# A streaming hybrid trunk on one core: norms folded into their neighbour stages, keys, values and queries in one stage, and longer tile loads for the delta rule

## The chip, the cores and the metric

The kernel runs on one core of one Trainium2 chip. The metric is the device time of one execution in microseconds (us), the median of several runs. The profile is one execution of the same program.

## The reference

1024 prompt frames and 64 sample frames (1088 tokens, width 1024) go through two layers, in fp32. Cut to what matters here:

```python
def _rmsnorm(x, g):
    return x * rsqrt(mean(x * x) + EPS) * g

# layer 0: gated delta rule in chunks of 64 tokens, then a dense FFN
proj = _rmsnorm(x, norm_attn[0]) @ gdn_w_in          # conv, silu, l2norm give q, k, v; z, gates
sol = triangular_solve(a, rhs)                       # per chunk and head, 64 x 64
v_new = u - w @ S
o = (q * exp(g)) @ S + attn @ v_new
S = S * exp(g_last) + k.T @ v_new
x = x + (_rmsnorm(o, o_norm) * silu(z)) @ gdn_w_out
h = _rmsnorm(x, norm_ffn[0]);  x = x + (silu(h @ w1) * (h @ w3)) @ w2

# layer 1: sliding-window attention with one shared K/V, then a top-2-of-8 expert FFN
kv = _rmsnorm(x, kv_norm) @ w_kv                     # k is rotated
q = rope(_rmsnorm(x, norm_attn[1]) @ swa_w_q)
x = x + attend(q, k, v) @ swa_w_o
x = x + moe(_rmsnorm(x, norm_ffn[1]));  y = _rmsnorm(x, final_norm)
```

## The kernel before

The program is a row of stages; each allocates its own tiles and ends in a barrier of all engines. The activations stay in SBUF as `xT` (128 partitions, 8 tiles of 1088 tokens: feature by token). A product of a weight tile and the activations runs over three token blocks of 384, 384 and 320 columns into one PSUM bank each. Most products are `split_product` (line 178): weight and activations are each split in a rounded fp32r half and a remainder, and three fast passes are added (lines 182 to 184).

The stages in order: load, norm0, gates, projection, **delta**, mixout, tails, **norm1**, **ffnup**, ffndown, **norm2**, **kv heads**, values, **norm3**, **q heads**, attend, attout, norm4, routing, experts, final.

*Delta* (`delta_stage`) walks 17 chunks of 64 tokens in two chains of 4 head pairs. Every engine runs the same hand-written order of steps per chunk, `ORDER`, in which the steps x0, d0, x1, d1, vT and kT prepare the next chunk and R0 to R3 work on this one:

```python
ORDER = ("R0", "x0", "T", "d0", "R1", "x1", "R2", "d1", "R3", "vT", "N", "kT", "M")
```

x0 and x1 (PE line 1053) multiply the between-block scores `BT` with the solved triangular tile `TT`; d0 and d1 multiply the result with `TT` again (lines 1062 to 1064) and DVE subtracts it (line 1181). vT and kT turn v and k (lines 1072, 1079), R0 multiplies k and q with the state (line 1089), R1 to R3 make the new values, the new state and the output, and T gates the output of the chunk before. POOL scales the state (line 1030), copies gate columns (line 1022) and clears the next but one `TT` (line 1013). SP loads everything, in order: per tile of 128 tokens 16 DMAs for v, k (twice), q and z (`load_tile`, lines 933 to 937); per chunk 16 DMAs of 16x8x16 for the diagonal blocks of `TT` (line 962), one for `BT` (line 943) and one for the scores (line 949). `TT` and `BT` have two buffers each. Every second chunk the tile load stands ahead of the next solved tile:

```python
for c in range(NCHUNK):
    if c and c % 2 == 0:
        ...
        store_out(c // 2 - 1)
        if c // 2 + 1 < NT:
            load_tile(c // 2 + 1)
    if c + 2 < NCHUNK:
        load_solved(c + 2)
        load_between(c + 2)
        load_own(c + 2)
```

Before the first chunk DVE does the substitution of the last group of blocks (15 dependent pairs of small operations, lines 432 and 433); the result goes to DRAM and is loaded as the last chunk's `TT`.

*norm_stage* squares `xT` on ACT (line 272), adds pairs on DVE, sums over the partitions with a product by ones on PE (line 288), takes Ln and Exp on ACT, and DVE multiplies `xT` by gain and inverse norm (line 304). For ffnup it also splits the result in halves (lines 281 and 308); norm3 reuses norm2's inverse norm. *ffn_up_stage* loads two weight tiles per step (SP line 1289), POOL casts and splits them (lines 189, 191), PE does 44 products (two for each of 22 tiles), ACT takes Silu from PSUM (line 1320) and DVE multiplies it with the other product (line 1336). *add_product_stage* (mixout, ffndown, attout) splits its weights with ACT and POOL (lines 1411, 1388) and adds PSUM to `xT` on DVE (line 1439). *heads_stage* is called twice, 4 tiles for kv and 8 for q, with plain fp32 products (PE line 1501), whole weights loaded at its start (line 1481), ACT copying PSUM out (lines 1513, 1514), a product with a permutation for the rotation (line 1488), and DVE multiplying by cosine and sine (lines 1525 to 1530).

## Time and profile before

| what | us |
|---|---|
| runs (3) | 5010.85 to 5026.13, median 5025.32 |
| the profiled execution | 5010.89 |
| its span in the profile | 5009.2 |
| PE, DVE, ACT, POOL busy | 4260.1, 1897.7, 1629.8, 781.3 |
| delta stage, first load to last instruction | 829 to 1316 |
| norm1, from its first ACT instruction | 1563.0 |
| ffnup, first load to last product of DVE | 1604.7 to 2149 |
| norm2 to the start of attend | 2468.6 to 2767.9 |
| experts | some 3120 to 4960 |

An engine's busy time counts its instructions; waits, register work and DMA issue don't count. A timeline row has the start, the duration, the engine with its line and operation, the tiles, the count of merged instructions, and in brackets the idle time before it with what released it. SP's rows are the issue of DMAs on its queue, not their transfer. A row of busy time by stretch has the window, its length, the busy time of PE, PEld (weight loads), DVE, ACT and POOL with their instruction counts, then PEclk (TensorE's granted clock as a share of full speed), the busy share of the DMA engines and GB/s.

### The profile page before, as it was taken

The numbers are of one execution on the slowest core, as the hardware profiler recorded it, in microseconds if no ns is written. First come the engines' busy times: TensorE is split into PE (matmuls) and PEld (weight loads), VectorE is DVE, ScalarE is ACT, GpSimd is POOL, SyncE is SP. The second block draws the span as 40 slices with busy tenths as digits, with TensorE's granted clock in tenths as the row PEclk, the third lists the DMA queues.
The fourth block names the chain that finished last, engine by engine and source line by source line (L and its number), as shares of the span: only waits on it lengthen the run. The fifth ranks groups of instructions, "written<-read, shape, count | busy, mean of one in ns | idle before, by whom it ended". The sixth has DMA issues, their size and how long they took to land. (4 is left out here: it accounts for less than half of the span.)

```text
span 5009.2 us, 84182 instructions
## 1 busy us (share of the span) xinstructions
PE 4260.1 (85%) x33144; PEld 4016.5 (80%) x33144; DVE 1897.7 (38%) x2635; ACT 1629.8 (33%) x2867; POOL 781.3 (16%) x567
## 2 busy tenths in 40 slices
PE   3899995767695999979769677399999999999994
PEld 2889995756695999979736456399999999999993
DVE  3455664544312000011112542144545445455553
ACT  2573331433322000022200442153434344444441
POOL 0334310211132222223200112200000000000001
PEclk7999997988897999989879788599999999999996
DMA  1223587454432222134120012555656666666675
GB/s 51 65 69 96 140 221 174 119 119 114 126 115 58 66 64 64 52 117 124 55 59 6 0 30 74 156 154 157 171 168 171 173 179 175 184 186 182 177 209 178
DMA packets 1048767, 600.88 MB, mean 120 GB/s; under 512 B 184466, under 2 KB 1006195, under 8 KB 1048579
## 3 DMA queue, kind: packets, MB, share of 16 engines
q1 hardware_dynamic: 984114, 524.46, 37.9%
q10 hardware_dynamic: 55344, 46.60, 3.2%
q0 software_dynamic: 9120, 27.24, 1.7%
q8 instruction: 127, 2.08, 0.2%
q14 instruction: 62, 0.50, 0.0%
HBM read 498.56 MB, written 99.26 MB: 119 GB/s over the span
## 5 line engine op out<-in xcount | busy, mean ns | idle before, releaser
L2260 DVE TENSOR_TENSOR experts_w<-experts_raw,experts_w 128x1024 fp32r<-128x1024 f32 x352 | 415.2, 1220 | 152.7 <-ACT experts_w L2220 152.6
L182 PE MATMUL experts_pa<-experts_hx,experts_w 128*128 128x264 f32 (+6 forms) x1408 | 412.3, 293 | 9.5 <-DVE experts_w L2260 9.5
L183 PE MATMUL experts_pa<-experts_hx,experts_w 128*128 128x264 f32 (+6 forms) x1408 | 410.8, 292 | 0.0
L184 PE MATMUL experts_pa<-experts_hx,experts_w 128*128 128x264 f32 (+6 forms) x1408 | 409.8, 291 | 0.0
L182 PE MATMUL experts_pd<-experts_hid,experts_w 128*128 128x264 f32 (+6 forms) x1408 | 409.7, 291 | 0.0
L183 PE MATMUL experts_pb<-experts_hx,experts_w 128*128 128x264 f32 (+6 forms) x1408 | 409.3, 291 | 0.0
L182 PE MATMUL experts_pb<-experts_hx,experts_w 128*128 128x264 f32 (+6 forms) x1408 | 408.6, 290 | 0.0
L183 PE MATMUL experts_pd<-experts_hid,experts_w 128*128 128x264 f32 (+6 forms) x1408 | 408.4, 290 | 0.0
L184 PE MATMUL experts_pb<-experts_hx,experts_w 128*128 128x264 f32 (+6 forms) x1408 | 408.2, 290 | 0.0
L184 PE MATMUL experts_pd<-experts_hid,experts_w 128*128 128x264 f32 (+6 forms) x1408 | 408.1, 290 | 0.0
L182 PE MATMUL proj_pm<-hT,proj_w_hi 128*128 128x384 f32 (+1 forms) x1152 | 389.0, 338 | 19.7 <-POOL proj_w_lo L630 19.7
L184 PE MATMUL proj_pm<-hT,proj_w_lo 128*128 128x384 f32 (+1 forms) x1152 | 380.9, 331 | 0.0
L182 PE MATMUL ffnup_pm<-h_ffn,ffnup_w_hi 128*128 128x384 f32 (+1 forms) x1056 | 346.4, 328 | 39.7 <-POOL ffnup_w_lo L191 39.7
L183 PE MATMUL proj_pm<-hT,proj_w_hi 128*128 128x384 f32 (+1 forms) x1152 | 378.6, 329 | 0.0
L2220 ACT ACTIVATE experts_w<-experts_raw 128x1024 fp32r<-128x1024 f32 x352 | 351.9, 1047 | 16.2 <-DMA experts_raw<-in_moe_w 15.7
L184 PE MATMUL ffnup_pm<-h_ffn,ffnup_w_lo 128*128 128x384 f32 (+1 forms) x1056 | 348.6, 330 | 0.0
L183 PE MATMUL ffnup_pm<-h_ffn,ffnup_w_hi 128*128 128x384 f32 (+1 forms) x1056 | 346.9, 329 | 0.0
L2274 DVE TENSOR_TENSOR experts_w<-experts_raw,experts_w 128x1408 fp32r<-128x1408 f32 x128 | 202.3, 1622 | 199.3 <-ACT experts_w L2233 199.3
L182 PEld LDWEIGHTS experts_pa<-experts_hx,experts_w 128*128 128x128 f32 x1408 | 266.3, 189 | 10.0 <-DVE experts_w L2260 6.9
L183 PEld LDWEIGHTS experts_pa<-experts_hx,experts_w 128*128 128x128 f32 x1408 | 266.3, 189 | 0.0
L184 PEld LDWEIGHTS experts_pa<-experts_hx,experts_w 128*128 128x128 f32 x1408 | 266.2, 189 | 0.0
L184 PEld LDWEIGHTS experts_pb<-experts_hx,experts_w 128*128 128x128 f32 x1408 | 264.8, 188 | 0.0
(385 smaller groups left out, 10013.1 us busy)
## 6 DMA issues: line engine op xcount, KB each, us to landing
experts_raw<-in_moe_w SPq DMA_DIRECT2D x352, 512.0 KB, 4.7
experts_raw<-in_moe_w SPq DMA_DIRECT2D x128, 704.0 KB, 5.7
projected<-proj_out SPq DMA_DIRECT2D x48, 544.0 KB, 4.1
proj_w<-in_gdn_w_in ACTq DMA_DIRECT2D x48, 512.0 KB, 4.1
ffnup_w<-in_ffn_w SPq DMA_DIRECT2D x44, 512.0 KB, 5.0
ffndown_w<-in_ffn_w SPq DMA_DIRECT2D x32, 704.0 KB, 4.5
mixout_w<-in_gdn_w_out SPq DMA_DIRECT2D x32, 512.0 KB, 3.8
hidden<-ffnup_hid ACTq DMA_DIRECT2D x22, 544.0 KB, 2.7
```

The lines of the kernel that those rows point to most:

```text
L182: pe.matmul(out, as_r(w_hi), as_r(x_hi), start=first, stop=False)
L183: pe.matmul(out, as_r(w_hi), as_r(x_lo), start=False, stop=False)
L184: return pe.matmul(out, as_r(w_lo), as_r(x_hi), start=False, stop=last)
L2220: act.activation(as_r(w[:, u, 0, x, 0:KD, :]), raw[:, x, u, 0:KD, :], ACT.Copy).then_inc(rounded[x][u], 1)
L2260: dve.tensor_tensor(as_r(w[:, u, 1, x, 0:KD, :]), raw[:, x, u, 0:KD, :], w[:, u, 0, x, 0:KD, :], ALU.subtract).then_inc(split[x][u], 1)
L2274: dve.tensor_tensor(as_r(w[:, u, 1, x, :, :]), raw[:, x, u, :, :], w[:, u, 0, x, :, :], ALU.subtract).then_inc(split[x][u], 1)
```

## The change

1. **Delta.** v, q with k, and z of a tile become three DMAs of 1 MB; the first tile and the incoming states are issued from ACT's queue at the start of the stage. POOL copies v and k (k twice) per chain and chunk into the layouts that the transposes want. `TT` and `BT` get three buffers (`AHEAD`), and their loads are issued three chunks ahead. The substitution of the last group is spread, two steps per chunk over chunks 1 to 8, and its store moves to the pass of chunk 11 in SP's loop.
2. **Adding stages.** After each addition to `xT` DVE squares the sum and adds it to a tile `squares`.
3. **ffnup.** norm1 goes. `inverse_norms` sums `squares` over the partitions on PE, ACT takes the root, DVE the reciprocal. ACT rounds `xT` times gain and DVE makes the remainder; the inverse norm is multiplied in when DVE takes the products out of PSUM. The first step of PE's loop is written out with waits for each split tile.
4. **Heads.** norm2 and norm3 go. kv and q are one stage of 12 tiles with `split_product`; POOL multiplies the weights by the gain, ACT rounds them, POOL makes the remainder; DVE multiplies by the inverse norm on the way out of PSUM. Weights come tile by tile, in two buffers.

The diff, cut to its core:

```diff
 # delta_stage
-        BT = st.sb("BT", [P, 2, L, HK, CHUNK])
-        TT = st.sb("TT", [P, 2, 2, HK, CHUNK])
+        BT = st.sb("BT", [P, AHEAD, L, HK, CHUNK])
+        TT = st.sb("TT", [P, AHEAD, 2, HK, CHUNK])
...
+            def load_tile(eng, t):
+                par, n = t % 2, TILES[t][1]
+                for to, first, loaded in ((v, 2 * HK, v_loaded), (qk, 0, qk_loaded), (z, 2 * HK + HV, z_loaded)):
+                    eng.dma_start(to[:, par, :, 0:n], proj[first:first + HV, :, t * P:t * P + n].rearrange("h p t -> p h t")).then_inc(loaded[par], 16)
...
+                load_between(0)
                 load_solved(0)
...
+                load_between(2)
+                load_solved(2)
+                load_tile(sp, 1)
                 for c in range(NCHUNK):
...
                         if c // 2 + 1 < NT:
-                            load_tile(c // 2 + 1)
+                            load_tile(sp, c // 2 + 1)
...
+                    if c + AHEAD < NCHUNK:
+                        load_between(c + AHEAD)
+                        load_solved(c + AHEAD)
                     if c + 2 < NCHUNK:
-                        load_solved(c + 2)
-                        load_between(c + 2)
                         load_own(c + 2)
...
+                    t = tile(c)
+                    pool.wait_ge(v_loaded[t], landed(c))
...
+                    pool.tensor_copy(vst[ch][:, c % 2, :, :], v[:, t, HC * ch:HC * ch + HC, cols(c)]).then_inc(e["v_staged"], 1)
+                    pool.wait_ge(qk_loaded[t], landed(c))
+                    pool.tensor_copy(kst[ch][:, c % 2, :, :, :], qk[:, t, HK + PAIRS * ch:HK + PAIRS * ch + PAIRS, cols(c)].unsqueeze(2).broadcast_to([P, PAIRS, 2, CHUNK])).then_inc(e["k_staged"], 1)
...
+                load_tile(act, 0)
+                for ch in C:
+                    act.dma_start(S[ch][:, 1, :, :], io["state_delta"][0, 0, HC * ch:HC * ch + HC].rearrange("h k v -> k h v")).then_inc(sems[ch]["state_loaded"], 16)
...
-                substitute(dve, step, blocks, solved, terms, 1)
...
+                    substitute(dve, step, blocks, solved, terms, 1, 2 * c - 1, min(2 * c + 1, SUB))
 # inverse_norms (new)
+        for b, (c, n) in enumerate(BLK):
+            last = pe.matmul(bank[:, b, 0:n], m["const"][:, C_ONES * P:(C_ONES + 1) * P], m["squares"][:, c:c + n], start=True, stop=True)
...
+            last = act.activation(root[:, c:c + n], bank[:, b, 0:n], ACT.Sqrt, bias=m["eps"][:, :], scale=1.0 / D)
...
+        dve.reciprocal(rinv[:, :], root[:, :]).then_inc(inverted, 1)
 # ffn_up_stage, ACT and DVE
+                for k in range(KD):
+                    act.activation(as_r(hT[:, 0, k, :]), m["xT"][:, k, :], ACT.Copy, scale=by_gain(k)).then_inc(x_rounded, 1)
+                    if k == 1:
+                        roots(act)
...
+                    dve.scalar_tensor_tensor(out=as_r(hT[:, 1, k, :]), in0=m["xT"][:, k, :], scalar=by_gain(k), in1=hT[:, 0, k, :],
+                                             op0=ALU.mult, op1=ALU.subtract).then_inc(x_split, 1)
+                    if k == 3:
+                        invert(dve)
...
+                    dve.tensor_tensor(two, rtwo, pm[:, x, 0:2, 0:384], ALU.mult)
+                    dve.tensor_tensor(rest, rrest, pm[:, x, 2, 0:320], ALU.mult).then_inc(scaled_now, 1)
 # add_product_stage, DVE
+                    dve.tensor_tensor(sq[:, :].rearrange("p (b t) -> p b t", b=2), to, to, ALU.mult).then_inc(squared, 1)
...
+                    dve.tensor_tensor(own, own, sq[:, :], ALU.add).then_inc(gathered, 1)
 # heads_stage, POOL, PE and ACT
+                    pool.tensor_tensor(w[:, u, :, :], w[:, u, :, :], m["gains"][:, gain:gain + KD].unsqueeze(2).broadcast_to([P, KD, P]), ALU.mult).then_inc(w_gained[u], 1)
+                    pool.wait_ge(w_rounded[u], PRE + t // 2 + 1)
+                    pool.tensor_tensor(as_r(w_lo[:, u, :, :]), w[:, u, :, :], w_hi[:, u, :, :], ALU.subtract).then_inc(w_split[u], 1)
...
+                            last = split_product(pe, pm[:, u, b, 0:n], w_hi[:, u, k, :], w_lo[:, u, k, :], xs[:, 0, k, c:c + n], xs[:, 1, k, c:c + n], k == 0, k == KD - 1)
...
+                    act.activation(as_r(xs[:, 0, k, :]), m["xT"][:, k, :], ACT.Copy).then_inc(x_rounded, 1)
+                    if k == 0:
+                        weights(0)
+                    if k == 1:
+                        roots(act)
```

Three places in the order of the instructions. On SP, in the loop over the chunks of the delta stage, the end of one tile load and what follows it, before:

```order
L933 DMA delta_vst<-projected 128x8x64
L935 DMA delta_kst<-projected 128x4x64 x2
L933 DMA delta_vst<-projected 128x8x64
L935 DMA delta_kst<-projected 128x4x64 x2
L936 DMA delta_qst<-projected 128x4x128
L937 DMA delta_zst<-projected 128x8x128
L962 DMA delta_TT<-solved_blocks 16x8x16 x16
L943 DMA delta_BT<-between_blocks 128x1024
L949 DMA delta_attn<-own_scores 128x512
L962 DMA delta_TT<-solved_blocks 16x8x16 x16
L943 DMA delta_BT<-between_blocks 128x1024
L949 DMA delta_attn<-own_scores 128x512
```

Here the block pieces of the next tile stand behind the whole tile load. The same place in the change, one pass of two chunks:

```order
L968 DMA gated_outputs<-delta_out 128x8x128 x2
L935 DMA delta_v<-projected 128x16x128
L935 DMA delta_qk<-projected 128x16x128
L935 DMA delta_z<-projected 128x16x128
L944 DMA delta_BT<-between_blocks 128x1024
L963 DMA delta_TT<-solved_blocks 16x8x16 x16
L950 DMA delta_attn<-own_scores 128x512
L944 DMA delta_BT<-between_blocks 128x1024
L963 DMA delta_TT<-solved_blocks 16x8x16 x16
L950 DMA delta_attn<-own_scores 128x512
```

Eight of the sixteen tile DMAs show in the first piece; the three in the second are a whole tile, and `BT` now stands ahead of the sixteen pieces, which belong to a chunk further on.

On POOL, two chunks of the delta stage before (`delta_S` is the state, `delta_cst` the gate columns):

```order
L1030 TENSOR_TENSOR delta_S<-delta_S,glast 128x1024 x2
L1022 COPY delta_cst<-cols 128x20 x2
L1013 MEMSET delta_TT 128x1024
L1030 TENSOR_TENSOR delta_S<-delta_S,glast 128x1024 x2
L1022 COPY delta_cst<-cols 128x20 x2
L1013 MEMSET delta_TT 128x1024
```

That is three kinds of work per chunk. One chunk of the same loop in the change:

```order
L1041 TENSOR_TENSOR delta_S<-delta_S,glast 128x1024 x2
L1025 COPY delta_cst<-cols 128x20
L1031 COPY delta_vst<-delta_v 128x512
L1033 COPY delta_kst<-delta_qk 128x512
L1025 COPY delta_cst<-cols 128x20
L1031 COPY delta_vst<-delta_v 128x512
L1033 COPY delta_kst<-delta_qk 128x512
L1016 MEMSET delta_TT 128x1024
```

Four copies per chunk stand between the state's scaling and the clearing of a `TT`.

On DVE, the end of norm1 and the head of ffnup's loop before:

```order
L304 SCALAR_TENSOR_TENSOR norm_h<-xT,gains,norm_rinv 128x1088
L308 TENSOR_TENSOR h_ffn<-norm_h,h_ffn 128x1088
L304 SCALAR_TENSOR_TENSOR norm_h<-xT,gains,norm_rinv 128x1088
L308 TENSOR_TENSOR h_ffn<-norm_h,h_ffn 128x1088 x2
L265 UNCONDITIONAL_BRANCH
L1327 UNCONDITIONAL_BRANCH
L1329 UNCONDITIONAL_BRANCH
L1329 ISA
L1332 ISA
L1333 ISA
L1336 TENSOR_TENSOR ffnup_hid<-ffnup_silu,ffnup_pm 128x768
L1337 TENSOR_TENSOR ffnup_hid<-ffnup_silu,ffnup_pm 128x320
```

The loop has one step, two instructions, per tile. The same place in the change:

```order
L1404 SCALAR_TENSOR_TENSOR h_ffn<-xT,gains,h_ffn 128x1088 x4
L1316 RECIPROCAL ffnup_rinv<-ffnup_root 128x1088
L1404 SCALAR_TENSOR_TENSOR h_ffn<-xT,gains,h_ffn 128x1088 x4
L1409 UNCONDITIONAL_BRANCH
L1409 ISA
L1412 REGISTER_ALU
L1399 TENSOR_TENSOR ffnup_scaled<-ffnup_rinv,ffnup_pm 128x768
L1400 TENSOR_TENSOR ffnup_scaled<-ffnup_rinv,ffnup_pm 128x320
L1414 REGISTER_ALU
L1399 TENSOR_TENSOR ffnup_scaled<-ffnup_rinv,ffnup_pm 128x768
L1400 TENSOR_TENSOR ffnup_scaled<-ffnup_rinv,ffnup_pm 128x320
L1419 ISA
```

The multiplications by the inverse norm have moved behind the products, and a reciprocal of 128x1088 stands in the middle of the splits.

## Rows read from the trace of the kernel before

**Rows 1.** Busy time by stretch: delta's start, delta, ffnup.
```profile
829.00:882.00 53.00, 11.52 (x176) 10.83 (x176) 12.05 (x38) 1.54 (x4) 2.99 (x6) 0.55 0.90 191
882.00:1316.00 434.00, 313.47 (x5675) 283.13 (x5673) 203.78 (x402) 171.70 (x677) 82.47 (x81) 0.88 0.48 114
1618.00:2152.00 534.00, 529.20 (x3168) 528.94 (x3166) 29.72 (x44) 39.20 (x55) 135.91 (x42) 1.00 0.20 62
```

**Rows 2.** PE's waits by line, delta stage: us in total, times, longest.
```profile
PE delta_bank_x L1053 <- issue: 104.8, 15, 14.7
```

**Rows 3.** Timeline of PE, delta stage: start, us, instruction, [idle before <-releaser].
```profile
840.30 1.97 PE L1053 MATMUL delta_bank_x<-delta_TT,delta_BT 64*64 64x64 f32 x32 [27.68 <-DMA delta_BT<-between_blocks]
...
845.02 0.45 PE L1062 MATMUL delta_bank_x<-delta_X,delta_TT 64*64 64x64 f32 x4
...
875.52 1.98 PE L1053 MATMUL delta_bank_x<-delta_TT,delta_BT 64*64 64x64 f32 x32 [29.83 <-DVE delta_TT L1181]
...
882.55 1.09 PE L1089 MATMUL delta_bank_w<-delta_S,delta_kst 128*64 128x128 f32 x16 [0.28 <-DVE delta_kd L1194]
...
900.44 1.09 PE L1089 MATMUL delta_bank_w<-delta_S,delta_kst 128*64 128x128 f32 x16
...
919.91 1.09 PE L1089 MATMUL delta_bank_w<-delta_S,delta_kst 128*64 128x128 f32 x16
...
957.61 1.97 PE L1053 MATMUL delta_bank_x<-delta_TT,delta_BT 64*64 64x64 f32 x32 [14.63 <-issue]
...
1297.86 1.09 PE L1089 MATMUL delta_bank_w<-delta_S,delta_kst 128*64 128x128 f32 x16
```

**Rows 4.** Timeline of SP's queue, delta stage.
```profile
928.69 1.36 SPq L933 DMA_DIRECT2D delta_vst<-projected  x1
...
945.79 8.05 SPq L962 DMA_DIRECT2D delta_TT<-solved_blocks  x16
```

**Rows 5.** Timelines of ACT, SP, POOL and PE around norm1 and ffnup.
```profile
1563.00 4.11 ACT L272 ACTIVATE norm_sq<-xT 128x1088 f32<-128x1088 f32 x4 [18.36 <-PEq L144]
...
1604.70 20.32 SPq L1289 DMA_DIRECT2D ffnup_w<-in_ffn_w  x8
...
1610.87 1.89 POOL L189 CAST ffnup_w_hi<-ffnup_w 128x2048 fp32r<-128x2048 f32 x1 [63.76 <-DMA ffnup_w<-in_ffn_w]
...
1617.46 0.68 PE L182 MATMUL ffnup_pm<-h_ffn,ffnup_w_hi 128*128 128x384 f32 x1 [39.74 <-POOL ffnup_w_lo L191]
```

**Rows 6.** Timelines of ACT, PE and DVE, norm2 to attend.
```profile
2468.55 4.11 ACT L272 ACTIVATE norm_sq<-xT 128x1088 f32<-128x1088 f32 x4 [18.59 <-PEq L144]
...
2511.90 20.11 PE L1501 MATMUL kv_pm<-h_att,kv_w 128*128 128x384 f32 x60 [27.61 <-DMA kv_w<-in_w_kv]
...
2577.10 0.73 DVE L1537 COPY vTt<-kv_raw 128x1088 f32<-128x1088 f32 x1 [13.83 <-ACT kv_raw L1514]
...
2597.56 10.19 DVE L304 SCALAR_TENSOR_TENSOR h_att<-xT,gains,rinv_att 128x1088 f32<-128x1088 f32 x8 [5.34 <-PEq L144]
...
2646.39 1.99 PE L1488 MATMUL q_pm<-q_raw,const 128*128 128x384 f32 x6
...
2767.87 0.63 ACT L1733 ACTIVATE attend_qs<-qT 128x512 f32<-128x512 f32 x1 [8.62 <-PEq L144]
```

**Rows 7.** Timeline of DVE, start of the delta stage.
```profile
865.40 0.16 DVE L432 TENSOR_TENSOR delta_terms<-delta_solved,delta_blocks 128x1 f32<-128x1 f32 x1 [36.76 <-DMA delta_blocks<-score_blocks]
```

**Rows 8.** Groups by line and shape, whole span: busy us, mean ns | idle.
```profile
L630 POOL TENSOR_TENSOR proj_w_lo<-proj_w,proj_w_hi 128x1024 fp32r<-128x1024 f32 x48 | 148.6, 3096 | 184.2 <-ACT proj_w_hi L656 183.0
...
L1388 POOL TENSOR_TENSOR mixout_w_lo<-mixout_w,mixout_w_hi 128x1024 fp32r<-128x1024 f32 x32 | 76.2, 2385 | 167.1 <-ACT mixout_w_hi L1411 167.1
...
L1705 POOL COPY attend_ks<-kT 128x384 f32 x12 | 7.7, 640 | 112.0 <-PE attend_scores L1653 112.0
...
L405 DVE RECIPROCAL gates_beta<-gates_beta 128x144 f32<-128x144 f32 x1 | 1.1, 1054 | 0.0
...
L1336 DVE TENSOR_TENSOR ffnup_hid<-ffnup_silu,ffnup_pm 128x768 f32<-128x768 f32 x22 | 21.0, 954 | 516.7 <-PE ffnup_pm L184 516.7
```

More of the change, by code:

```diff
@@ L423, in _, with substitute @@
                         dve.tensor_copy(rows[:, a, s:s + n], pchan[0:HV, b, 0:n]).then_inc(emptied, 1)
-def substitute(dve, step, blocks, solved, terms, groups):
-    for i in range(1, SUB):
+def substitute(dve, step, blocks, solved, terms, groups, first=1, end=SUB):
+    for i in range(first, end):
         t = terms[:, 0:groups * i * i].rearrange("p (g c j) -> p g c j", c=i, j=i)
@@ L1099, in v_new @@
                     for i, hp in both:
-                        last = pe.matmul(b_w[ch][rows(hp), i, :], TT[rows(hp), par, 1, PAIRS * ch + i, :], vb[ch][rows(hp), i, :], start=True, stop=True)
+                        last = pe.matmul(b_w[ch][rows(hp), i, :], TT[rows(hp), slot, 1, PAIRS * ch + i, :], vb[ch][rows(hp), i, :], start=True, stop=True)
                     last.then_inc(e["vn_summed"], 1)
@@ L1301, in _, with product @@
             def _(pe):
-                with pe.Fori(0, KF // 2) as i:
+                def product(i, u, x, freed, done, first=False):
+                    pe.wait_ge(freed, PRE + 2 * i + u)
+                    for k in range(KD):
+                        if first:
+                            pe.wait_ge(x_split, PRE + k + 1)
+                        for b, (c, n) in enumerate(BLK):
+                            last = split_product(pe, pm[:, x, b, 0:n], w_hi[:, u, x, k, :], w_lo[:, u, x, k, :], hT[:, 0, k, c:c + n], hT[:, 1, k, c:c + n],
+                                                 k == 0, k == KD - 1)
+                    last.then_inc(done, 1)
@@ new lines, in _ @@
+                dve.wait_ge(inverted, PRE + 1)
+                dve.wait_ge(rope_l, PRE + 16)
+                for t in range(HEAD_TILES):
+                    dve.wait_ge(done, PRE + t + 1)
+                    if not rotated(t):
+                        dve.sem_inc(copied, 1)
+                        scale(vT[:, t - KV_T, :], t).then_inc(ready, 1)
+                        continue
+                    if t >= 2:
+                        dve.wait_ge(ready, PRE + t - 1)
+                    scale(raw(t), t).then_inc(copied, 1)
+                    dve.wait_ge(copied, PRE + t + 1)
+                    dve.wait_ge(turned, PRE + rotations(t) + 1)
+                    two, rest = blocks3(sn)
+                    stwo, srest = blocks3(rope[:, 1, :])
+                    dve.wait_ge(ready, PRE + t)
+                    dve.tensor_tensor(two, stwo, pm[:, t % 2, 0:2, 0:384], ALU.mult)
+                    dve.tensor_tensor(rest, srest, pm[:, t % 2, 2, 0:320], ALU.mult)
+                    step(dve.tensor_tensor(raw(t), raw(t), rope[:, 0, :], ALU.mult))
+                    for to, c in dests(t):
+                        n = to.shape[-1]
+                        last = dve.tensor_tensor(to, raw(t)[:, c:c + n], sn[:, c:c + n], ALU.add)
+                    last.then_inc(ready, 1)
```

378 lines of the change are left out of this document (214 added, 164 removed).

## Prediction

> **What bounds the kernel now.** I read four views in this order: busy time by stretch, the PE waits by line in the delta stage, and then the timelines of the engines where one stage hands over to the next.
>
> By stretch [rows 1] the stages differ. In the up projection PE is busy 529 of 534 us at a granted clock of 1.00, so that stage can only lose its start or its end: 529.20 us over 3168 matmuls is 0.167 us each, and the 72 of one product take **12.03 us**. In the delta stage PE is busy 313 of 434 us, DVE 204, POOL 82, and the DMA engines 0.48 of the time: nothing there is full, so something waits in line. Of the waits of that stage [rows 2] one dominates: 104.8 us, in 15 pieces of up to 14.7 us, in front of the first between-block product (L1053), with no releaser that the profile names.
>
> The PE timeline [rows 3] shows where. R0 of successive chunks (L1089, the mark I count periods with) starts at 882.55, 900.44, 919.91; then the L1053 product at 957.61 has waited 14.63. From the first R0 to the last at 1297.86 there are 16 periods in 415.31 us, 25.96 each, while the undisturbed one from 900.44 to 919.91 takes 19.47. SP [rows 4] explains it: at 928.69 it starts the small loads of the next tile (16 DMAs) and only at 945.79 the 16 block pieces of the solved tile, 8.05 us of issue, without which L1053 can't start. 945.79 + 8.05 is 953.84, and a few us of landing later PE goes on, at 957.61. SP's issue, 17.1 us for one tile, is the wait.
>
> The norms are serial [rows 5, 6]. Norm1 starts at 1563.00, the first weight DMA of the up stage goes out at 1604.70 and PE's first product at 1617.46, so 54.5 us pass without a product. From norm2 at 2468.55 to attend at 2767.87 there are 299.3 us: two norms, loads of weights that nothing covers (PE waits 27.61 before its first product there, at 2511.90), and 12 tiles at fp32.
>
> **The change part by part.**
>
> *Delta, the start.* x0 runs at 840.30 now; it waits for the same transfers afterwards. Its update ends at 845.47 (the last d0 group starts at 845.02), and DVE's subtraction follows in some 0.7 us. Today x1 waits till 875.52, 29.83 us on DVE [rows 3], because DVE first has the substitution of the last group, which itself waits 36.76 us for its blocks [rows 7] and runs from 865.40 to about 874.5. Without it x1 could run at 846.7 and R0 7.03 us later, at 853.7 (from 875.52 to 882.55). What is late next is the tile: v and qk, 2 MB, come from ACT's queue beside SP's loads. At the 191 GB/s of this stretch [rows 1], half of it for ACT, 2 MB land some 22 us after 829, at 851, and the copies, the transposes and the scaling of k come behind. I take R0 at 856, with bounds 853.7 and 865: **−26.5** (−28.9 to −17.6).
>
> The rule that would speak against moving these loads is in the Trainium skill, Trainium Kernel Development and Optimization, Key Constraints: DMAs of all issuing queues share the same 16 engines, and another queue saves issue time only. The DMA share of 0.90 in this stretch [rows 1] agrees. By that rule alone the start keeps its bytes, only their order helps, and the gain would be the lower end, −17.6, in place of −26.5.
>
> *Delta, the periods.* SP's queue for a pair of chunks now holds 2 stores, 3 loads, and twice BT, 16 pieces and attn, and the pieces are those of three chunks ahead. Issue of the pieces is 2 × 8.05; with some 5 us for the rest that is 21 of two periods' 38.9 us, so SP is no limit, and one chunk more of lead covers the landing. I take 19.47 for each of 16 periods, 311.5: **−103.8**. Ends: the first period, 17.89 (882.55 to 900.44; it lacks the gate of an earlier chunk, so I don't take it), −129; and 20.5, one more us of staging in every period, −87.
>
> *What is added there.* POOL copies v and k for both chains, 4 of 128x512 per chunk. The nearest row is a copy of 128x384 at 640 ns [rows 8], so 0.85 each, 3.4 per chunk, at most 6 if the broadcast of k is dear. POOL is busy 82 of 434 us, 4.9 per chunk; 8.3 of 19.5 is covered. The copies stand behind the two state scalings in POOL's order, and a late tile would hold the scalings and the clearing of the next chunk; PE needs v only in the last third of a chunk. The substitution becomes at most 1.8 us per chunk in 8 chunks of DVE, which is busy 204 of 434: **0**. Without that cover it costs its 9.1 us.
>
> *The up projection's start.* Its weight load moves from 1604.70 to norm1's place, 1563.00: **−41.7** [rows 5]. From load to first product stay 12.8 us. In that time ACT rounds 8 tiles (norm1's four took 4.11 us), PE sums the squares and DVE splits 8 (1.35 each, 954 × 1088/768 [rows 8]) with the reciprocal of 128x1088 after four. That one has a row only as 128x144 at 1054 ns [rows 8]: × 1088/144 is **8.0 us**. The last split comes about 1583; PE, from 1575.7 at 1.5 us per k and slower at first, would want it at about 1586. So the first product should hardly stall; I take 2, with ends 0 and 12 (the reciprocal in full and half as much again). The squares add 1.5 behind the last addition (two 128x544 operations at 954 × 544/768 = 0.68, and a hand-over), and the extra eviction step 1.4 behind the last product. Inside the loop the evictions run beside the other bank's product, some 4.1 of every 24 us of DVE, free. Sum: −41.7 + 2 + 1.5 + 1.4 = **−36.8** (−39 to −27).
>
> *Keys, values and queries.* From the old 2468.55: 1.5 for the squares; first weights 0.5 MB, about 4.8 us (two such take 6.17 in the up stage, 1604.70 to 1610.87), then POOL's gain 2.39, ACT's rounding of some 1.1 and POOL's difference 2.39 [rows 8], 11 in all; the first tile 20, since ACT's rounding of the weights stands in front of its later x tiles and the reciprocal falls into it; 11 more tiles × 12.03 = 132.3, three fast passes in place of fp32; 9 swaps of 2.0 [rows 6] = 18; behind the last product scaling, swap and rotation 7.5; and the values stage with its barriers as now, 2577.83 to 2597.56 [rows 6], 19.7. Sum 210.0 against 299.3: **−89.3** (−99 to −72). Each tile's weights take about 11 us to prepare, beside the 14 us of the tile ahead.
>
> *The attention output* also gathers squares, which nobody reads: **+1.5**.
>
> Sum: −26.5 − 103.8 − 36.8 − 89.3 + 1.5 = **−254.9**. On the profiled execution, 5010.9 us: 4756. The median of the three runs lies 14.4 above that, the lowest run at it; I put the forecast about midway, **4762 us**.
>
> **The rivals.**
>
> *The long waits stay.* No row names the releaser of the 104.8 us; that it is SP's issue is my reading of two timelines. Were it the landing of the transfers, or did the 3 MB now ahead of the pieces in the queue hold them, −103.8 would go: 4866. Against it: a DMA share of 0.48, and the sum 953.84 plus landing. 8 in 100.
>
> *POOL and DVE take turns at the stage starts.* The same subtraction of 128x1024 takes POOL 3096 ns in the projection, where DVE is busy, and 2385 in the mix output [rows 8]: so a cost of 0.7 each is seen. If at both starts POOL (6.6 in the up stage, 1610.87 to 1617.46 [rows 5], 4.8 in the heads) and DVE (eight splits of 1.35 each) ran one after the other, and the reciprocal came on top, up to 11 us each time and 6 for a clock that falls meanwhile: +28, 4790. 9 in 100. The Trainium skill, SBUF — State Buffer, Who interferes with whom, states such a rule: a VectorE operation with two SBUF inputs and a GpSimd operation that reads SBUF hold a shared port for the whole instruction. The 0.7 us of those rows agrees in sign and shows no full turn.
>
> *TensorE falls to 1.2 GHz.* Now the evictions of the up stage go through one more engine step. If PE waited for each, its granted clock could stay at the lower of its two levels and a product take up to twice as long: 44 × 12.03 = +529, 5291. It decides the sign from 21 slow products on (255/12). Against it: two PSUM banks, 4.1 of 24 us, and a clock of 1.00 now. 2 in 100; this is the case on the slow side.
>
> **How the numbers follow.** My forecast has 81 in 100, the three rivals 8, 9 and 2. The forecast's own ends, all costs at their better or worse bounds, are some −45 and +50, and not all at once: 4762 − 44 to 4762 + 58, **4718 to 4820**, takes in the second rival and leaves out the first and third, and perhaps one tenth more for several terms off together. Faster by over 0.3% (15 us, about what a measurement tells from no change): 0.97; within it 0.01; slower 0.02.
>
> **What would show it.** Right: R0 every 19.5 us, no wait of over 2 us before the first between-block product, R0 first near 856; the up stage's first weight DMA at the end of the tails stage and the first product 13 us later; heads at 14 us per rotated tile. Wrong: a pair of a long and a short period; PE waiting for POOL's copies or for DVE's reciprocal for more than a few us; a granted clock under 0.9 in the up stage.

## The result and the profile after

| | before | changed |
|---|---|---|
| median of 4 runs (us) | 5024.62 | 4770.62 |
| lowest and highest | 5010.85, 5026.13 | 4744.34, 4783.22 |
| profiled execution | 5010.89 | 4772.82 |

The ratio is 0.9497, with a 95% interval of 0.9473 to 0.9521: 5% faster. One execution of those reported below (the kernel before with attend filled, 6091.88 us at a mean granted clock of 0.676) was in a slow state and counts in no ratio. The forecast was 4762 in 4718 to 4820. Six marks in the two profiled executions show where the 238.0 us of their spans come from (starts in us; the first two columns are rows, the others differences):

| mark | before | changed | earlier by | gained since the mark above | forecast |
|---|---|---|---|---|---|
| first R0 of delta | 882.55 | 857.06 | 25.5 | 25.5 | 26.5 |
| last R0 | 1297.86 | 1154.78 | 143.1 | 117.6 | 103.8 |
| last addition of ffndown | 2465.30 | 2287.83 | 177.5 | 34.4 | 36.8 |
| attend's first ACT instruction | 2767.87 | 2501.95 | 265.9 | 88.4 | 89.3 |
| attout's first weight DMA | 2955.48 | 2714.24 | 241.2 | **−24.7** | 0 |
| end of the span | 5009.2 | 4771.2 | 238.0 | −3.2 | −1.5 |

Everything up to attend gained 9.5 us more than forecast; attend, which the change doesn't touch, gave back 24.7.

Busy time by stretch of the changed kernel (delta's start, delta, ffnup; columns as in [rows 1]):

```profile
831.00:857.00 26.00, 8.95 (x176) 7.92 (x176) 4.58 (x10) 1.53 (x4) 7.14 (x11) 0.64 1.11 258
857.00:1174.00 317.00, 297.78 (x5672) 269.54 (x5672) 221.24 (x432) 168.89 (x677) 119.22 (x144) 0.99 0.61 153
1436.00:1969.00 533.00, 530.29 (x3168) 529.77 (x3167) 107.08 (x116) 38.62 (x33) 155.82 (x42) 1.00 0.20 61
```

The delta stage takes 317 us in place of 434, and PE is busy 298 of them at a clock of 0.99, not 0.88. Its work is the same, so of the 117 us some 16 are PE's own time at the higher clock (313.5 us before, 297.8 now), which came with the end of the long waits; the rest was waiting. ffnup is as full as before: 530 of 533 us. PE's two largest waits in delta, which answer [rows 2]:

```profile
PE delta_bank_x L1064 <- DMA delta_TT<-solved_blocks: 31.1, 1, 31.1
PE delta_bank_w L1083 <- DVE delta_o L1233: 5.6, 32, 0.2
```

The 104.8 us ahead of the first between-block product are gone; what is left is the wait for the first pieces at the start. PE's timeline in delta, against [rows 3]:

```profile
847.21 1.98 PE L1064 MATMUL delta_bank_x<-delta_TT,delta_BT 64*64 64x64 f32 x32 [31.14 <-DMA delta_TT<-solved_blocks]
...
857.06 1.09 PE L1102 MATMUL delta_bank_w<-delta_S,delta_qk 128*64 128x128 f32 x16 [0.23 <-issue]
...
874.97 1.09 PE L1102 MATMUL delta_bank_w<-delta_S,delta_qk 128*64 128x128 f32 x16
...
893.67 1.09 PE L1102 MATMUL delta_bank_w<-delta_S,delta_qk 128*64 128x128 f32 x16
...
1154.78 1.09 PE L1102 MATMUL delta_bank_w<-delta_S,delta_qk 128*64 128x128 f32 x16 [0.16 <-issue]
```

R0 now comes every 18.6 us (297.72 over 16), mostly every 18.43. SP's queue: the first load of the tile ahead of it, then one whole tile load, against [rows 4]:

```profile
861.25 0.44 SPq L935 DMA_DIRECT2D delta_v<-projected  x1
...
902.50 1.36 SPq L935 DMA_DIRECT2D delta_v<-projected  x1
903.90 4.07 SPq L935 DMA_DIRECT2D delta_qk<-projected  x1
908.01 3.47 SPq L935 DMA_DIRECT2D delta_z<-projected  x1
911.58 3.49 SPq L944 DMA_DIRECT2D delta_BT<-between_blocks  x1
915.11 9.73 SPq L963 DMA_DIRECT2D delta_TT<-solved_blocks  x16
```

Here is the first thing that the prediction had wrong: three DMAs and `BT` keep SP from 902.50 to 915.07, 12.6 us, not some 5. The issue of a megabyte with only small pieces just ahead of it took 0.44 us (861.25); the second and third megabyte of a tile took 1.8 to 5.0 us each in this stage. Still nobody waits, because the pieces belong to a chunk three further on.

The start of ffnup, on ACT, SP, POOL, DVE and PE, against [rows 5]:

```profile
1421.56 2.29 ACT L1381 ACTIVATE h_ffn<-xT,gains 128x1088 fp32r<-128x1088 f32 x2 [21.31 <-PEq L144]
...
1422.19 73.70 SPq L1341 DMA_DIRECT2D ffnup_w<-in_ffn_w  x12
...
1428.16 1.89 POOL L189 CAST ffnup_w_hi<-ffnup_w 128x2048 fp32r<-128x2048 f32 x1 [25.09 <-DMA ffnup_w<-in_ffn_w]
1430.13 5.43 POOL L191 TENSOR_TENSOR ffnup_w_lo<-ffnup_w,ffnup_w_hi 128x2048 fp32r<-128x2048 f32 x1
...
1422.79 2.62 DVE L1404 SCALAR_TENSOR_TENSOR h_ffn<-xT,gains,h_ffn 128x1088 fp32r<-128x1088 f32 x2 [5.74 <-ACT h_ffn L1381]
1428.17 8.54 DVE L1404 SCALAR_TENSOR_TENSOR h_ffn<-xT,gains,h_ffn 128x1088 fp32r<-128x1088 f32 x2 [2.77 <-ACT h_ffn L1381]
1436.63 6.94 DVE L1316 RECIPROCAL ffnup_rinv<-ffnup_root 128x1088 f32<-128x1088 f32 x1
...
1435.62 0.69 PE L182 MATMUL ffnup_pm<-h_ffn,ffnup_w_hi 128*128 128x384 f32 x1 [10.07 <-POOL ffnup_w_lo L191]
...
1444.80 0.45 PE L182 MATMUL ffnup_pm<-h_ffn,ffnup_w_hi 128*128 128x384 f32 x1 [0.76 <-DVE h_ffn L1404]
```

From the load to PE's first product are 13.4 us (forecast 12.8). Two splits take 2.62 us at 1422.79 and 8.54 at 1428.17, and these end at 1436.71, one split's time behind the end of POOL's subtraction at 1435.56: the rows fit engines that took full turns. The reciprocal takes 6.94 us (estimated at 8.0). PE waits just 0.76 for a split, since it has four to work on meanwhile. But its first product starts when POOL's subtraction ends, and that took 5.43 us where the kernel before has

```profile
1612.84 4.49 POOL L191 TENSOR_TENSOR ffnup_w_lo<-ffnup_w,ffnup_w_hi 128x2048 fp32r<-128x2048 f32 x1
```

The heads stage, from its start to attend, against [rows 6]:

```profile
2293.66 1.11 ACT L1651 ACTIVATE x_halves<-xT 128x1088 fp32r<-128x1088 f32 x1 [21.18 <-PEq L144]
...
2302.86 0.69 PE L182 MATMUL heads_pm<-x_halves,heads_w_hi 128*128 128x384 f32 x1 [5.38 <-POOL heads_w_lo L1613]
...
2316.58 0.69 PE L182 MATMUL heads_pm<-x_halves,heads_w_hi 128*128 128x384 f32 x1 [5.43 <-DVE x_halves L1671]
...
2324.99 0.95 DVE L1666 TENSOR_TENSOR qT<-heads_rinv,heads_pm 128x768 f32<-128x768 f32 x1 [4.87 <-PE heads_pm L184]
...
2501.95 0.63 ACT L1891 ACTIVATE attend_qs<-qT 128x512 f32<-128x512 f32 x1 [8.78 <-PEq L144]
```

The first product starts 9.2 us into the stage (forecast 11) and the first tile takes 22.1 (forecast 20), with a wait of 5.43 for a split behind the reciprocal. By mark, 88.4 of the forecast 89.3.

Attend, before and changed, in the same columns as [rows 1]:

```profile
2767.87:2955.48 187.61, 131.59 (x1312) 85.49 (x1312) 106.75 (x272) 96.38 (x372) 21.65 (x49) 0.81 0.00 0
```

```profile
2502.00:2714.24 212.24, 163.22 (x1312) 105.48 (x1312) 109.82 (x273) 96.64 (x373) 20.20 (x49) 0.63 0.00 0
```

The same 1312 matmul records take 131.6 us of PE in one and 163.2 in the other; the granted clock is 0.81 and 0.63, and the stage 187.6 and 212.2 us.

### The profile page after: what moved, and what is told of

It is laid out like the page before. It is cut to its first block and busy times, and to the rows that moved or that the text cites. A ratio compares the mean times of both kernels' runs of the same rounds, so it can differ in the third digit from the quotient of the medians.

```text
span 4771.2 us, 84925 instructions
## 1 busy us (share of the span) xinstructions
PE 4231.1 (89%) x33396; PEld 4048.8 (85%) x33396; DVE 2130.2 (45%) x2800; ACT 1610.8 (34%) x2821; POOL 899.3 (19%) x659
## 5 line engine op out<-in xcount | busy, mean ns | idle before, releaser
L182 PE MATMUL proj_pm<-hT,proj_w_hi 128*128 128x384 f32 (+1 forms) x1152 | 389.2, 338 | 19.3 <-POOL proj_w_lo L630 19.3
L2378 ACT ACTIVATE experts_w<-experts_raw 128x1024 fp32r<-128x1024 f32 x352 | 351.9, 1047 | 17.1 <-DMA experts_raw<-in_moe_w 16.7
```

The lines of the kernel that those rows point to most:

```text
L182: pe.matmul(out, as_r(w_hi), as_r(x_hi), start=first, stop=False)
L2378: act.activation(as_r(w[:, u, 0, x, 0:KD, :]), raw[:, x, u, 0:KD, :], ACT.Copy).then_inc(rounded[x][u], 1)
```

## The experiments

Three questions stood: is attend's loss the change's doing; is it the number of loads or the lead (how many chunks ahead the pieces are issued) that took the wait out of delta; and what do the new stage starts cost.

### Attend's clock

**The changed kernel again.**

> The changed kernel once more, beside the kernel before. In the first profile attend took 187 us before (2767.87 to 2955.48) and 212 after (2502 to 2714) with the same instructions, at granted clocks of 0.58 to 0.95 before and 0.50 to 0.71 after. Theory A, the clock of attend differs from one execution to the next whatever stands ahead of it: attend somewhere between 185 and 215 us, time between 4744 and 4783. Theory B, the new heads stage ahead of attend holds the clock down: attend at 210 us or more again and a time of 4768 or more. If attend takes under 195 us, B falls.

Measured: 4756.88 (4750.58 to 4764.45), and attend took 198.6 us at a clock of 0.72. It lies between the two earlier values: neither of B's marks came (210 us, 4768), but it is above the 195 at which B was to fall, so this run alone decides nothing.

**Only the delta stage changed** (the kernel before with `substitute`, `delta_chunks` and `delta_stage` of the changed one).

> The kernel before with the change's delta stage only (long loads, three buffers, copies on POOL, substitution spread). Theory, the delta part gives back by itself what the trace of after shows (first R0 25.5 us earlier, 16 periods of 18.6 in place of 26.0): last R0 some 143 us earlier, time about 4882 beside a median of 5025 (or 4868 beside the best run). Rival, part of that gain comes from the rest of the change: less than 120 us. On attend: by theory A (its clock differs by execution) between 185 and 215 us; by theory B (the new heads stage lowers it) about 187, since the old heads stand ahead of it here.

**Only the norms and heads changed** (the changed kernel with those three functions of the one before).

> The changed kernel with the old delta stage: the squares, the up projection without norm1 and the joined heads stage only. Theory, the parts add up: the stretches from the end of delta to the start of ffnup's loads some 40 us shorter, norm2 to attend some 91 us shorter, time about 122 under the kernel before, 4903. Rival, POOL and DVE taking turns and the reciprocal cost more where the delta stage leaves other state: less than 105 us. On attend: theory A 185 to 215 us, theory B 210 or more.

Measured: 4886.22 (4878.03 to 4893.52) and 4916.55 (4886.61 to 4926.15), ratios to the kernel before of 0.9732 [0.9702, 0.9762] and 0.9804 [0.9773, 0.9836]. With delta alone the last R0 starts at 1151.04, 146.8 earlier. With the norms alone 265.0 us pass from the last R0 to ffnup's first load (1299.52 to 1564.56), 41.8 fewer than before, and 213.9 from ffndown's last addition to attend (2431.44 to 2645.3), 88.7 fewer. By these marks both theories of the parts hold. The medians say less: beside the 5014.95 us of the kernel before in the same session, delta alone gains 128.7 and the norms alone 98.4, under the 105 that stood for the rival, with an interval whose ends lie on both sides of a 2% gain. The runs of the norms alone spread over 40 us, and the profiled one is the fastest of them. Attend in the one and in the other:

```profile
2623.70:2835.51 211.81, 163.10 (x1312) 105.38 (x1312) 110.05 (x272) 95.41 (x372) 20.06 (x49) 0.62 0.00 0
```

```profile
2645.30:2829.71 184.41, 127.66 (x1312) 82.98 (x1312) 106.57 (x272) 97.88 (x373) 21.63 (x49) 0.83 0.00 0
```

With the old heads ahead of it attend took 211.8 us, with the new heads 184.4. Theory B falls: what the change put ahead of attend doesn't set its clock. Without attend, the profiled spans are 4821.6 us (5009.2 − 187.6) before, 4680.1 with delta alone, 4700.5 with the norms alone and 4559.0 with both: −141.5, −121.1 and −262.6. The parts add up, to the last digit by chance (the runs of one kernel spread far more), and the forecast for these stages, 254.9, was 7.7 short.

**Attend filled.** Four products that nobody reads go into attend where PE waits for the turned probabilities to be copied:

```diff
                     last.then_inc(e["p_turned"], 1)
+                    if not isinstance(i, int) or i >= 2:
+                        pe.wait_ge(e["o_copied"], PRE + i - 1)
+                    for x in range(4):
+                        pe.matmul(po[:, par, 2 * jp, :], ident, ident, start=True, stop=True, skip_group_check=True)
                     pe.wait_ge(e["v_staged"], PRE + i + 1)
                     pe.wait_ge(e["p_copied_a"], PRE + 2 * i + jp + 1)
                     pe.wait_ge(e["p_copied_b"], PRE + 2 * i + jp + 1)
-                    if not isinstance(i, int) or i >= 2:
-                        pe.wait_ge(e["o_copied"], PRE + i - 1)
```

> The changed kernel with four more products of 128x128 by 128 columns per step of attend (ident by ident, into the output's bank ahead of the products that overwrite it), where PE waits for the copies of the turned probabilities. Theory C, attend's clock falls because PE idles there: the granted clock of attend at 0.9 or more and its time at 180 to 190 us in spite of 34 x 4 more products, 4745 in all. Rival D, the extra products lie on the path and the clock does as it likes: attend at 215 to 250 us, 4790 or more.

Measured: 4735.60, and the four runs lie within 4734.14 to 4738.25, where those of the changed kernel spread over 39 us. Ratio 0.9438 [0.9410, 0.9466]. Attend:

```profile
2503.30:2679.10 175.80, 142.90 (x1584) 108.41 (x1584) 107.61 (x273) 97.80 (x373) 20.79 (x49) 0.95 0.00 1
```

175.8 us at a clock of 0.95, under the 180 to 190 expected, with 272 more matmul records (two for each of the 136 products) and 20 us less of PE than the changed kernel needed for the fewer. The edit also moves the wait for `o_copied` ahead of three others; that alone was not tried. Theory C stands: PE idled there, its clock was granted at the lower of its two levels for part of the stage (0.50 all through 2628 to 2700 in the changed kernel), and how large a part differed from run to run.

**The kernel before, filled the same way.**

> The kernel before with the four products per step in attend and nothing else. Theory C, attend's clock is its own matter and has nothing to do with the change: attend 174 to 178 us as in the filled changed kernel, time about 5011 - 187.6 + 176 = 4999, and runs within 6 us of each other where those of before spread by 26. Rival: attend stays at 185 or more, or the runs spread as before.

Measured: 4996.39 beside 5022.85, ratio 0.9952 [0.9930, 0.9973], and attend as foreseen:

```profile
2756.80:2932.13 175.33, 142.59 (x1584) 108.11 (x1584) 107.74 (x272) 96.69 (x372) 20.91 (x49) 0.95 0.00 1
```

The clock is attend's own matter. The runs did not draw together to within 6 us: nine of the ten lie between 4987 and 5008, 21 us apart, where those of the kernel before beside them spread over 42. So attend is not the only part of the kernel before that varies. Its delta stage, full of waits and at a clock of 0.88 [rows 1], may be another; that was not tried.

### Delta: number of loads or lead

Four kernels in pairs. Two buffers and a lead of two in place of three:

```diff
-AHEAD = 3
+AHEAD = 2
...
-                load_between(2)
-                load_solved(2)
```

and 16 DMAs for a tile in place of 3, with the same bytes and runs:

```diff
-                for to, first, loaded in ((v, 2 * HK, v_loaded), (qk, 0, qk_loaded), (z, 2 * HK + HV, z_loaded)):
+                for to, first, loaded, count in ((v, 2 * HK, v_loaded, 8), (qk, 0, qk_loaded, 4), (z, 2 * HK + HV, z_loaded, 4)):
```

> The changed kernel with two buffers of TT and BT and their loads two chunks ahead, as before; the three long tile loads stay. Changed kernel: 16 periods of R0 in 297.7 us. Theory S (SP's issue of the many small loads was the wait): with 3 loads for a tile SP's queue holds the next pieces back by 5 us only, so the periods stay within 298 to 330. Theory L (the lead of three chunks is what took the wait away, since the pieces queue behind 3 MB of tile whatever the number of DMAs): 370 to 415 again, with waits of 8 us or more ahead of the first between-block product in every second chunk.

> The changed kernel with every tile loaded by 16 DMAs (v in 8, q with k in 4, z in 4, the same bytes and runs) in place of 3; three buffers and the lead of three chunks stay. Theory S: SP issues about 17 us for a tile, 16.5 for two sets of pieces and 3 for the rest, 36.5 of a pair's 37.2 us, so it just fits: 298 to 340 for 16 periods. Theory L: the lead covers it, 298 to 302.

> Both undone: 16 DMAs per tile, two buffers and a lead of two chunks. Both theories: the old alternation of a short and a long period, 16 periods in 390 to 420 us, the long wait of some 14 us ahead of the first between-block product back in every second chunk. If it stays under 350, the copies to POOL or the longer runs took the wait away, and both fall.

Measured, 16 periods of R0 (their first and last in each timeline of PE):

| | 3 DMAs per tile | 16 DMAs per tile |
|---|---|---|
| lead of three | 297.7 | 295.3 |
| lead of two | 375.0 | 378.7 |

The number of DMAs does nothing that can be told here; the lead does it. The kernel that tells S from L is the one with long loads and a lead of two (at most 330 by S, 370 or more by L); with 16 DMAs and a lead of three both theories allowed 298 to 302, and 295.3 came. The times agree: 4832.53 and 4864.62 us with a lead of two, 4743.99 with 16 DMAs and a lead of three (one run each, each with its own attend). SP, POOL and PE with a lead of two and long loads:

```profile
904.23 1.35 SPq L935 DMA_DIRECT2D delta_v<-projected  x1
905.63 3.86 SPq L935 DMA_DIRECT2D delta_qk<-projected  x1
909.53 3.66 SPq L935 DMA_DIRECT2D delta_z<-projected  x1
913.30 3.48 SPq L944 DMA_DIRECT2D delta_BT<-between_blocks  x1
917.16 8.28 SPq L963 DMA_DIRECT2D delta_TT<-solved_blocks  x16
...
905.10 0.95 POOL L1014 MEMSET delta_TT<- 128x1024 f32 x1 [1.26 <-PE delta_bank_w L1111]
...
926.84 1.98 PE L1062 MATMUL delta_bank_x<-delta_TT,delta_BT 64*64 64x64 f32 x32 [9.29 <-issue]
```

`TT` is clear at 906.05, but its pieces are issued from 917.16 on, behind the tile, and PE waits 9.29 us for them. The tile with 16 DMAs took SP about as long:

```profile
903.73 6.36 SPq L938 DMA_DIRECT2D delta_v<-projected  x8
910.13 2.12 SPq L938 DMA_DIRECT2D delta_qk<-projected  x4
912.29 3.69 SPq L938 DMA_DIRECT2D delta_z<-projected  x4
916.08 0.94 SPq L947 DMA_DIRECT2D delta_BT<-between_blocks  x1
```

903.73 to 917.02 is 13.3 us, against 12.9 for three (904.23 to 917.16). So theory S falls as written: SP's time for a tile goes by what has to be moved, not by how many instructions ask for it. The expectation of the last kernel is missed too: undoing both gives 378.7, not the old 415, and a longest wait of 13.1 in place of 14.7. The difference of 37 us to the kernel before is one of waits ahead of the first between-block product (104.8 us there, 68.0 here). The old load also fetched k twice and v and k in runs of half the length, and had `BT` behind the pieces; which of these, or POOL's copies, took the 37 us away was not tried.

The lead works on the clock too. Over the 16 periods PE is busy 298.8 us at a clock of 0.90 with long loads and a lead of two, and 285.1 at 1.00 with a lead of three, so of the 77 us between them some 14 are PE's own time and 65.0 are waits.

**The pieces ahead of the tile**, with two buffers:

```diff
                         store_out(c // 2 - 1)
-                        if c // 2 + 1 < NT:
-                            load_tile(sp, c // 2 + 1)
...
                         load_between(c + AHEAD)
                         load_solved(c + AHEAD)
+                    if c and c % 2 == 0 and c // 2 + 1 < NT:
+                        load_tile(sp, c // 2 + 1)
```

> Two buffers and a lead of two chunks with three long tile loads, and SP's queue in another order: BT and the 16 pieces ahead of the tile load in every second chunk. With the tile load ahead of them the lead of two took 16 periods of R0 in 375 us, with three buffers 297.7. Theory Q (what counts is how much stands in SP's queue between the clearing of TT and its pieces; a third buffer and another order are two ways to the same): no wait over 3 us ahead of the first between-block product, 16 periods in 298 to 325, the rest above 298 from POOL's copies, which now wait for a later tile. Theory R (two buffers are too few whatever the order, since TT is cleared too late): the waits stay at 6 us or more and the periods at 350 or more.

Measured: 4771.81 us (one run), 16 periods in 322.9, inside Q's range; the longest wait ahead of the first between-block product is 3.1, where Q said no more than 3:

```profile
906.75 8.90 SPq L963 DMA_DIRECT2D delta_TT<-solved_blocks  x16
915.70 1.49 SPq L935 DMA_DIRECT2D delta_v<-projected  x1
...
927.72 0.61 POOL L1031 COPY delta_kst<-delta_qk 128x512 f32<-128x512 f32 x1 [4.31 <-DMA delta_qk<-projected]
...
941.53 1.80 PE L1062 MATMUL delta_bank_x<-delta_TT,delta_BT 64*64 64x64 f32 x32 [3.13 <-issue]
```

The pieces leave as soon as `TT` is clear, at 906.73; POOL then waits 4.31 for the tile that comes later. So two thirds of what the third buffer brings (52 of 77 us) could be had by order alone: R stands refuted, and the cause of these 77 us is settled. The wait was the pieces' place in SP's queue, behind 3 MB of tile.

**The substitution back at the start.** DVE does it in one go ahead of the chunks:

```diff
-                delta_chunks({"x": last_group, "d": d, ...
+                dve.wait_ge(blocks_loaded, PRE + 16)
+                substitute(dve, step, blocks, solved, terms, 1)
+                dve.tensor_copy(flipped[:, 0, :, :], solved[:, 0, :, :].rearrange("p r c -> p c r")).then_inc(flip_ready, 1)
+                delta_chunks({"x": skip, "d": d, ...
```

> The changed kernel with the substitution of the last group back ahead of the chunks on DVE (its blocks are loaded fourth now, at about 849). Changed kernel: first R0 at 857.1, 16 periods 297.7, three of them 19.1 to 19.6 where the others are 18.4. Theory: the first R0 moves to between 866 and 869 (the 9.1 us of substitution behind the landing of the blocks), and the three longer periods become 18.4, since in them a product of DVE with two SBUF operands waits for POOL's state scaling (1.62 us in place of 0.27): 16 periods in 294 to 296. Rival: the longer periods come from late transfers and stay; or the first R0 moves by 25 us, as much as the change gained there.

Measured: 4751.41 us (one run); first R0 at 863.97, 6.9 later than in the changed kernel and a little less than expected; 16 periods in 296.9. The stage began 1.8 us earlier in this execution (SP's first load at 829.76). Counted from that load, the first R0 comes after 53.5 us in the kernel before, 34.2 here and 25.5 in the changed kernel. So some 19 us at the start come from the earlier loads (the blocks no longer queue behind a tile: issued at 841.33 in the changed kernel, 861.01 before), and 9 from the spreading. The longer periods stay (19.3, 19.2 and 18.8 in the same places), so the expectation missed there: DVE's waits beside POOL's scaling are not their cause. In each PE has a gap of this kind inside d0:

```profile
926.25 0.33 PE L1075 MATMUL delta_bank_x<-delta_TT,delta_X 64*64 64x64 f32 x4 [0.67 <-issue]
```

What holds PE there the trace doesn't name; it is 1 to 3 us in all and was left open.

### The stage starts

**Starts in another order**, on the filled kernel: in heads five x tiles are rounded ahead of the first weights, the reciprocal stands behind all splits in both stages, and attout gathers no squares.

```diff
-                    if k == 0:
-                        weights(0)
-                    if k == 1:
-                        roots(act)
+                    if k == 4:
+                        weights(0)
+                        roots(act)
...
-                    if k == 3:
-                        invert(dve)
+                invert(dve)
```

> The filled kernel with the starts put in another order: in the heads stage ACT rounds five x tiles ahead of the first weights, and takes the root behind them; there and in ffnup the reciprocal stands behind all eight splits; attout gathers no squares. In the changed kernel PE's first heads tile starts at 2302.86, waits 5.43 for a split at 2316.58 and ends at 2324.99. Theory: without the reciprocal in the middle the first tile takes 15 to 17 us and not 22, ffnup's start gains under 1 us (its wait there is 0.76), attout 3: some 9 us less than the filled kernel's 4735.6, 4725 to 4729. Rival: the reciprocal only moves, and PE's second tile or its first swap waits for the scaling instead: 4733 or more.

Measured: 4725.83 (4723.34 to 4729.17), 9.8 under the filled kernel, ratio to the kernel before 0.9409 [0.9370, 0.9447]; the lowest median of all. The two kernels ran on different chips and their ratios' intervals overlap, so the 9.8 is less sure than the rows. PE's first heads tile and DVE ahead of it, and DVE at the start of ffnup:

```profile
2300.66 0.69 PE L182 MATMUL heads_pm<-x_halves,heads_w_hi 128*128 128x384 f32 x1 [7.21 <-POOL heads_w_lo L1615]
...
2300.95 7.27 DVE L1672 TENSOR_TENSOR x_halves<-xT,x_halves 128x1088 fp32r<-128x1088 f32 x3 [2.55 <-ACT x_halves L1653]
...
2315.12 0.95 DVE L1667 TENSOR_TENSOR qT<-heads_rinv,heads_pm 128x768 f32<-128x768 f32 x1
...
1425.66 19.54 DVE L1404 SCALAR_TENSOR_TENSOR h_ffn<-xT,gains,h_ffn 128x1088 fp32r<-128x1088 f32 x6 [2.77 <-ACT h_ffn L1381]
```

The tile takes 14.5 us (2300.66 to its scaling at 2315.12) in place of 22.1, but starts 11.2 us into the stage (from 2289.46) and not 9.2, so 5.7 us are won. From the end of attend to the end of the span the filled kernel takes 2054.9 us and this one 2054.0: of the 3 us expected from attout's squares 0.9 shows. In ffnup six splits took 19.54 us, 11.7 more than at their own 1.31, beside POOL's two casts and subtractions; and PE did not wait for them. The rest of the 9.8 has no row.

**Eight products in attend in place of four**, on that last kernel.

> The same with eight products per step of attend in place of four. Theory C (a clock held up by activity): the granted clock in attend is at 0.95 with four already, so eight bring no more than 2 us of clock and put up to 34 x 4 x 0.28 = 38 us on PE, part of it on the path: attend 178 to 205 us in place of 176, time 2 to 25 us above the kernel with four. Rival: attend takes 170 us or less, PE's idle time hides all eight.

Measured: 4732.72, 6.9 above four; attend 183.3 us at a clock of 0.96, where four took 175.8 at 0.95. There is no more clock to win, and the products are on the path.

## Why the prediction came out right

*The total* was 4762 against 4770.6, with two errors of opposite sign. That it came within 9 us is partly luck: the four runs spread over 39 us, and the median of the same kernel in the next session was 4756.88. Delta's periods were put at 19.47 and are 18.61: 13.8 us better. The row that I called undisturbed wasn't: PE's timeline of the kernel before has a wait at x0 in that short period too, and the changed kernel has that period at 18.70 and most others at 18.43. That row was also taken at a clock of 1.00, where the whole stage before had 0.88, so the clock's share of the gain was in the forecast without being named.

```profile
905.14 1.15 PE L1053 MATMUL delta_bank_x<-delta_TT,delta_BT 64*64 64x64 f32 x32 [0.98 <-issue]
```

The other way, attend lost 24.7 us, a stage that I costed at nothing because its code is the same. Its clock is not the same: 0.81 in the profiled execution before, which was a lucky one, and 0.63 in the one after.

*The mechanism in delta* was half right. That R0's long periods were waits for the pieces behind a tile in SP's queue holds, by the lead-of-two kernels. That "SP's issue, 17.1 us for one tile, is the wait", to be cut by three DMAs to "some 5 us for the rest", fails: SP takes 12.6 us for the tile and `BT` in the changed kernel, and 16 DMAs with the same lead give 295.3 us. What I gave half a sentence, "one chunk more of lead covers the landing", did 77 of the 118 us; the rest came with the tile load and the copies, and was not taken apart. The rival "The long waits stay", by 3 MB ahead of the pieces in the queue, describes the lead-of-two kernel rightly: 8 waits of 65.0 us together there, 9.29 in the row shown.

*The start of delta*: −25.5 for −26.5. But x0 itself starts 6.9 us later than before (847.21 for 840.30): the stage began 2.5 us later in this execution (SP's first load at 831.53 for 829.06), and from the issue of the last piece to x0 pass 6.4 us with ACT's loads beside it, at a DMA share of 1.11 in the stretch. Less time passes from x0 to R0 than I had added up (9.9 against 13.4). Of the substitution, only some 9 us were to be had, by the kernel that puts it back. That the step came out right is luck in its parts. The Trainium skill, Trainium Kernel Development and Optimization, Key Constraints, has loads issued from several queues interleave on the same engines; that share and x0's delay agree with it, but no run took ACT's loads away.

*ffnup* gave 34.4 of 36.8: stage start and reciprocal were sized well, and the squares and handovers cost a little more. *Heads* gave 88.4 of 89.3, with parts up to some 2 us off in either direction (the first product earlier, the first tile longer). One sign of being wrong did show there: PE's 5.43 us for a split behind the reciprocal, which the forecast's 20 us for the first tile had nearly in it.

*The rival of turns on POOL and DVE* is real as a mechanism and small as a price. I had written that the rows of before show no full turn; those of after do, 8.54 us for 2.62. The rule of the Trainium skill, SBUF — State Buffer, Who interferes with whom, agrees with that row: a split with two SBUF inputs starts only when POOL's instruction ends. In ffnup it cost PE 0.76 us for a split and 0.9 in POOL's first subtraction, against 2 in the forecast. With the same code in another execution the first product came 14.6 us after the load, not 13.4. *The rival of a falling clock* named the wrong stage: ffnup stayed at 1.00, and it was attend, with the same code, that ran at a lower one.

## What to carry to other kernels

When a transfer is late, ask first what stands ahead of it in its queue and how early it could have been issued: a buffer more, or small urgent loads ahead of large ones, was worth 50 to 80 us here, and fewer DMAs for the same bytes nothing. A stage whose engine idles in short gaps can run at another clock in the next run with the same code; before a difference there is explained, look at the granted clock of that stage in several executions. Where an inverse norm is a factor of each column, it can be applied after the product, and then its latency runs beside the product and no longer ahead of it.

## What the runs showed of the hardware that I had not expected

- Attend's 1312 matmul records ran at mean granted clocks of 0.55 to 0.84 in the ten profiled executions that had its code unchanged, 184 to 222 us; with four unread products per step it was 0.95 in three kernels, 175.3 to 175.8 us. Work that nobody reads made the stage 9 to 46 us shorter.
- The issue of a 1 MB DMA on SP took 0.44 us with only small pieces just ahead of it and 1.8 to 5.0 us behind another megabyte in the same queue.
- A reciprocal of 128x1088 took 6.94 us on DVE, 6.4 ns per column, where 128x144 took 1054 ns [rows 8].
- A product on DVE of two SBUF operands of 128x64 took 1.62 us beside POOL's state scaling in the changed kernel and 0.27 in the kernel before:

```profile
916.60 1.62 DVE L432 TENSOR_TENSOR delta_terms<-delta_solved,delta_blocks 128x64 f32<-128x64 f32 x1
```

```profile
914.22 3.88 POOL L1041 TENSOR_TENSOR delta_S<-delta_S,glast 128x1024 f32<-128x1024 f32 x2 [9.89 <-PE delta_bank_s L1105]
```

It ends just as POOL's pair of scalings does, at 918.10 to 918.22.
